# Output projection of the second block in branch halves, with a third pair of banks for the key scores

## The reference, cut to what matters

```python
mixed = jnp.concatenate([rmsnorm(o_attn, norm_attn_g[l]), rmsnorm(o_conv, norm_conv_g[l])], axis=-1)
x = x + gt1 * (mixed @ w_out[l])
h2 = rmsnorm(x, ln_ffn_g[l]) * (1 + sc2) + sh2
x = x + gt2 * peer_ffn(h2, peer_wq[l], peer_keys[l], peer_u[l], peer_v[l])

def peer_ffn(xn, w_q, sub_keys, expert_u, expert_v):
    q = (xn @ w_q).reshape(B, S, PEER_HEADS, 2, PEER_QDIM // 2)
    s = jnp.einsum('bshpd,hpkd->bshpk', q, sub_keys)
    v_half, i_half = lax.top_k(s, PEER_TOPK)
    ...
```

## Time and profile before

| | |
|---|---|
| median of 3 runs | 1239.91 us (1239.68 to 1240.51) |
| the profiled execution's own time | 1240.15 us |
| its span in the profile | 1238.4 us |
| PE busy | 1193.9 us, 96% of the span |
| DVE, ACT, POOL busy | 74%, 63%, 46% |

### The profile page before, as it was taken

How to read it: one execution, slowest core, us unless ns; L and a number is a source line. 1 busy time by engine, 2 the same in 40 slices (tenths; PEclk the granted TensorE clock), 3 DMA queues, 4 the chain that set the end, 5 groups by cost and what they waited for, 6 DMA issues and landing times.

```text
span 1238.4 us, 26652 instructions
## 1 busy us (share of the span) xinstructions
PE 1193.9 (96%) x8256; PEld 1072.4 (87%) x8256; DVE 911.3 (74%) x1885; ACT 782.6 (63%) x1784; POOL 566.6 (46%) x505
## 2 busy tenths in 40 slices
PE   8999999988897999999999999999999999999997
PEld 8888988988877999888999999998888888888886
DVE  5777768889575739997788888861676767676866
ACT  5446676465765555667887788876655555555555
POOL 3665543435464348998877777778200000000000
PEclk9999999999999999999999999999999999999999
DMA  6668656538643445565666666667676676767663
GB/s 230 228 210 298 231 196 199 170 118 302 245 126 120 134 124 173 185 187 184 195 215 209 199 201 215 201 208 270 196 243 214 193 255 194 256 193 263 188 194 109
DMA packets 85828, 249.86 MB, mean 202 GB/s; under 512 B 8019, under 2 KB 29692, under 8 KB 84988
## 3 DMA queue, kind: packets, MB, share of 16 engines
q1 hardware_dynamic: 77356, 209.62, 53.6%
q0 software_dynamic: 8400, 39.34, 8.7%
HBM read 237.38 MB, written 13.12 MB: 202 GB/s over the span
## 4 chain that ended last, share of the span: by engine, by line
PE 82%; DVE 8%; issue 4%; ACT 3%; POOL 3%; DVEq 0%; POOLq 0%; ACTq 0%
PE psum L694 81%; POOL w_lo L1644 2%; DVE w_lo L1814 1%; DVE s_sb L1828 1%; ACT w_hi L1217 1%; DVE arena L1867 1%; DVE rstd L1808 0%; ACT arena L1376 0%; ACT arena L1200 0%; PE psum L895 0%; DVE arena L2023 0%; DVE arena L1982 0%; DVE xres L1948 0%; POOL arena L1727 0%; DVE arena L1929 0%
## 5 line engine op out<-in xcount | busy, mean ns | idle before, releaser
L694 PE MATMUL psum<-h_parts,w_hi 128*128 128x256 f32 (+1 forms) x3216 | 678.0, 304 | 22.0 <-DVE w_lo L1814 8.2
L1644 POOL TENSOR_TENSOR w_lo<-ring,w_hi 128x512 fp32r<-128x512 f32 x368 | 490.8, 1346 | 275.1 <-ACT w_hi L1217 266.6
L1217 ACT ACTIVATE w_hi<-ring 128x512 fp32r<-128x512 f32 x734 | 444.9, 628 | 255.8 <-PE psum L694 244.4
L694 PEld LDWEIGHTS psum<-h_parts,w_hi 128*128 128x128 f32 x3216 | 516.6, 192 | 58.8 <-issue 24.3
L694 PE MATMUL psum<-h_parts,w_lo 128*128 128x256 f32 x1832 | 518.0, 283 | 0.0
L694 PEld LDWEIGHTS psum<-h_parts,w_lo 128*128 128x128 f32 x1832 | 350.8, 191 | 0.0
L694 PE MATMUL psum<-w_hi,h_parts 128*128 128x512 f32 (+1 forms) x1120 | 342.7, 388 | 3.8 <-DVE w_lo L1814 2.5
L694 PEld LDWEIGHTS psum<-w_hi,h_parts 128*128 128x128 f32 x1120 | 208.4, 188 | 49.5 <-issue 6.3
L1814 DVE TENSOR_TENSOR w_lo<-ring,w_hi 128x512 fp32r<-128x512 f32 x238 | 189.3, 796 | 81.6 <-ACT w_hi L1217 81.0
L694 PE MATMUL psum<-w_lo,h_parts 128*128 128x512 f32 (+1 forms) x560 | 216.3, 386 | 0.0
L2341 DVE TENSOR_TENSOR w_lo<-ring,w_hi 128x512 fp32r<-128x512 f32 x128 | 88.5, 692 | 61.6 <-ACT w_hi L1217 58.2
(11 more groups left out here) (214 smaller groups left out, 1002.3 us busy)
## 6 DMA issues: line engine op xcount, KB each, us to landing
ring<-u_t SPq DMA_DIRECT2D x128, 512.0 KB, 3.6
ring<-v_rows SPq DMA_DIRECT2D x128, 512.0 KB, 3.7
ring<-weights SPq DMA_DIRECT2D x115, 512.0 KB, 3.9
arena<-mods POOLq DMA_DIRECT2D x48, 512.0 KB, 5.3
routing_weights<-s_sb SPq DMA_DIRECT2D x32, 320.0 KB, 4.2
s_sb<-routing_weights POOLq DMA_DIRECT2D x5, 2048.0 KB, 10.3
bias_rows<-bias_row POOLq DMA_DIRECT2D x1, 1536.0 KB, 10.8
xres<-x_t SPq DMA_DIRECT2D x2, 512.0 KB, 4.6
```

The lines of the kernel that those rows point to most:

```text
L694: return nc.tensor.matmul(out, lhs, rhs, start=start, stop=stop, **kw)
L1217: nc.scalar.activation(w_hi[:, half, :], src, ACT.Copy).then_inc(hi_done, 1)
L1644: nc.gpsimd.tensor_tensor(w_lo[:, half, :], src, w_hi[:, half, :].bitcast(F32), ALU.subtract)\
```

## The change

The output projection's slots no longer hold one column block with all its rows. Each holds the convolution rows of two blocks or the attention rows of two blocks, in the order of `OUT2`. PE multiplies the convolution halves of blocks 0 to 3 first, chunk by chunk over the four blocks, then their attention halves in the same manner, and then convolution and attention halves of blocks 4 and 5 and of 6 and 7. In `mix 0` DVE now splits each convolution chunk behind the scaling of the next one, where it did all four in `mix 1`. The key scores use banks 6 and 7 for part 2.

```diff
+OUT2 = [("conv", 0), ("conv", 1), ("attn", 0), ("attn", 1), ("conv", 2), ("attn", 2), ("conv", 3), ("attn", 3)]
+OUT2_AHEAD = (3, 3, 4, 5, 6, 7, 8, 8)
...
+        def key_banks(x):
+            return psum[:, 2 + 2 * (x % 3):4 + 2 * (x % 3), :]
...
+            if s[0] == "out2":
+                branch, pair = OUT2[i]
+                for b in range(2):
+                    n_half += branch == "conv"
+                    half_free[k, b] = (half_used, n_half) if branch == "conv" else (v_done, VT[s + (2 * pair + b,)] + 1)
+                continue
...
-            pair = s[0] in ("out2", "wq") and job == 0
+            if s[0] == "out2":
+                return SPLIT[SLOT_AT[s]] + OUT2_AHEAD[job]
+            pair = s[0] == "wq" and job == 0
...
+            def out2_half(branch, blocks):
+
+                ready, first = part_ready("out2"), branch == "conv"
+                for c4 in range(4):
+                    c = c4 + (0 if first else 4)
+                    for nb in blocks:
+                        n, k = VT["out2", nb], first_wq - KC + OUT2.index((branch, nb // 2))
+                        if c4 == 0:
+                            half_ready(k, nb % 2)
+                            if first:
+                                take_v(n)
+                        ready(c)
+                        last = split_mms(vbuf(n), (2 * k + nb % 2) % 4, c4 * P, (h_hi[:, c, :], h_lo[:, c, :]),
+                                         first and c4 == 0, not first and c4 == 3)
+                        if c4 == 3:
+                            last.then_inc(half_used if first else v_done, 1)
...
-                elif kind in ("out1", "out2"):
-                    if kind == "out2":
-                        split_pair(VT["out2", 0], first_wq - KC, part_ready("out2"), take_v, v_done, (1,))
-                    for nb in range(2 if kind == "out2" else 0, KC):
...
+                elif kind == "out2":
+                    out2_half("attn", range(4))
+                    for pair in (2, 3):
+                        out2_half("conv", (2 * pair, 2 * pair + 1))
+                        out2_half("attn", (2 * pair, 2 * pair + 1))
...
-                        split_pair(VT["out2", 0], first_wq - KC, part_ready("out2"), take_v, v_done, (0,))
+                        out2_half("conv", range(4))
...
-                        if x >= 2:
-                            pe_.wait_ge(key_read, x - 1)
+                        if x == 3:
+                            pe_.wait_ge(key_read, 1)
...
                     if j:
-                        low_parts("out2", range(4))
                         dve.wait_ge(o_ready, 8)
...
-                        if c and j:
-                            low_parts("out2", (3 + c,))
+                        if c:
+                            low_parts("out2", (4 * j + c - 1,))
...
+                dve.wait_ge(key_read, 3)
                 v.tensor_copy(top_v1, top_v[:, 1, :, :]).then_inc(picked, 1)
```

More of the change, by code:

```diff
@@ L546, in block_program @@
                 half_free[k, 1] = a_done, filled(*s, i)
-            elif s[0] in ("out1", "out2"):
+            elif s[0] == "out1":
                 half_free[k, 1] = v_done, VT[s + (i,)] + 1
@@ L949, in _ @@
                             last.then_inc(v_done, 1)
-                elif kind in ("out1", "out2"):
-                    if kind == "out2":
-                        split_pair(VT["out2", 0], first_wq - KC, part_ready("out2"), take_v, v_done, (1,))
-                    for nb in range(2 if kind == "out2" else 0, KC):
+                elif kind == "out1":
+                    for nb in range(KC):
                         split_projection(VT[s + (nb,)], SPLIT[SLOT_AT[s]] + nb, part_ready(kind), take_v, v_done)
+                elif kind == "out2":
[3 more added lines that the diff above has]
+                        out2_half("attn", (2 * pair, 2 * pair + 1))
                 elif kind == "gate":
@@ L1027, in _ @@
                                 pe_.wait_ge(a_read, filled("wq", hd))
-                                last = mm(psum[:, 2 + 2 * (x % 2) + m, j * P:j * P + P],
+                                last = mm(key_banks(x)[:, m, j * P:j * P + P],
                                           blk(QP + hd)[DH * m:DH * m + DH, P * i:P * i + P],
@@ L1081, in _ @@
             for s in range(4):
-                wide_tile(s, WIDE_FROM + s, WIDE_EARLY[s], (key_read, 3) if s >= 2 else (act_read, WIDE_FROM - 1 + s))
+                wide_tile(s, WIDE_FROM + s, WIDE_EARLY[s], (key_read, 4) if s >= 2 else (act_read, WIDE_FROM - 1 + s))
             wide_tiles(WIDE_FROM + 4, SEL_TILE, WIDE_EARLY, WIDE_FROM)
@@ L1465, in _ @@
                         act.wait_ge(key_done, x + 1)
-                        banks = psum[:, 2 + 2 * (x % 2):4 + 2 * (x % 2), :]
                         nc.scalar.activation(scores_of(i)[:, :, first:first + 4, :],
-                                             banks.rearrange("p m (j k) -> p m j k", j=4), ACT.Copy)\
+                                             key_banks(x).rearrange("p m (j k) -> p m j k", j=4), ACT.Copy)\
                             .then_inc(key_read, 1)
@@ L2516, in stream @@
             out[n] = w.reshape(16, P, DH).transpose(1, 0, 2).reshape(P, D)
+        elif k == "out2":
+            branch, pair = OUT2[i]
+            rows = wo2[0:512] if branch == "conv" else wo2[512:1024]
+            out[n] = np.concatenate([cols(rows[:, P * nb:P * nb + P]) for nb in (2 * pair, 2 * pair + 1)], 1)
         else:
-            w = {"out1": x["w_out"][0], "gate": x["w_ple_gate"][0], "out2": wo2, "wq": x["peer_wq_2"][0]}[k]
+            w = {"out1": x["w_out"][0], "gate": x["w_ple_gate"][0], "wq": x["peer_wq_2"][0]}[k]
             out[n] = cols(w[:, P * i:P * i + P])
```

## The result

The changed kernel took 1244.62 us in the median of 8 runs, the kernel before 1239.80 in the median of 8. The ratio is 1.0039, with a 95% interval from 1.0029 to 1.0048: **4.8 us slower** (3.6 to 6.0). The ratios are taken over all runs of a kernel, so they can differ in the last digit from those of two medians.

A forecast was written before the change was run, and what follows sets the result against it. PE was taken to bound the kernel (82% of the span). Stage +3.73, tail +0.8, key scores -1.04 and clock +1.8 sum to +5.3 on 1239.91, so 1245.2 us; range 1241.8 to 1248.0.

The forecast's parts named there:

- Start: Ahead of the output projection: the first low split moves ahead, so PE starts at 400.34, -0.57 us.
- Attention chunks 0.6 later: In `mix 0`, alternating scalings and splits delay the attention norm's reciprocal and all that follows by 0.6 us.
- First boundary: From convolution to attention halves of blocks 0 to 3: PE waits 2.45, 0.84 and 0.98 for weights, sum 4.27 us.
- Second boundary: Ahead of the convolution halves of blocks 4 and 5: PE waits 1.45 and 0.85 for weights, sum 2.3 us.
- Tail: Behind the stage's last group: DVE's last residual starts 1.2 us behind the stage's end; +0.8, bounds 0.6 to 1.0.
- Key scores: In `route`: part 2 fills PE's 1.47 us wait for the first copy out; -1.04 us, or 0 if lost.
- The clock: In the output projection: PE's clock falls to half after the waits; +1.8 us, with 0 to 3.
- The sum for the stage: Output projection: +3.73 us from start, full-rate groups and boundary waits, plus 1.8 for slow clock.
- the first (waits and no slow clock): Output projection: the waits come but no slow clock; +3.5, 1243.4 us; chance 0.20.
- the second (the refill hidden): First boundary: weights are in place when convolution halves end, waits 0 to 1 us; 1236.8 us at zero; chance 0.06.
- the fourth (a slow clock and waits at each later boundary): Later boundaries: cover fails, 0.3 to 0.7 us each for three, slow clock at each boundary; 1248 us; chance 0.07.
- The third (taken back later): Behind the stage: a later PE wait of 3 us or more absorbs the loss; 1239.9 us; chance 0.07.

The follow-up runs named there:

- tail: The changed kernel with the last attention halves multiplied block by block (6, then 7) instead of side by side; 1244.57 us, ratio 1.0041 to the kernel before.
- after_again: The changed kernel measured once more with no edit, for a profile at the usual speed; 1246.19 us, ratio 1.0049 to the kernel before.
- late_split: The changed kernel with DVE splitting the four convolution chunks behind all four scalings again; 1244.92 us, ratio 1.0043 to the kernel before.
- key_only: The kernel before with only the third pair of banks for the key scores added; 1238.88 us, ratio 0.9996.
- pairs_ahead_tail: The changed kernel with blocks 0 to 3 in pairs, slot 2 rounded ahead of the attention chunks, last attention halves block by block; 1239.05 us, ratio 0.9993.
- early_split: The kernel before with only the moved split of the convolution chunks, each behind the next chunk's scaling; 1241.36 us, ratio 1.0010.

## Why the prediction was right

The forecast was 1245.2 us, +5.3; the two measurements are +4.8 and +6.1, with intervals that hold +5.3. Step by step, from the profile of the changed kernel:

- *Start*: forecast -0.57; PE's idle time ahead of the stage is 2.21 instead of 2.82, -0.61.
- *Attention chunks 0.6 later*: the attention norm's root is 401.17 - 396.00 = 5.17 us behind the convolution's, and before it was 400.78 - 396.46 = 4.32. That is 0.85 later where I had 1.0 for this row. ACT's last attention cast, counted in the same way, is 0.5 later, where I had 0.6.
- *First boundary*: forecast 2.45, 0.84 and 0.98; measured 2.25, 0.78 and 0.25. The last one came out small since the groups ahead of the fourth already ran at the half clock and used up most of the wait; at 0.36 per group it would have been 410.72 - 409.04 - 2 x 0.36 = 0.96. POOL's two lows took 3.01 us, as the row of before (2.99) had it. The Trainium skill ("SBUF — State Buffer", section "SBUF: two separate sides") lets either DVE or POOL hold their shared port for a whole instruction; by that the estimate for these two lows and DVE's between them is 1.29 + 0.68 + 1.29 = 3.26, and the trace is 0.25 below it.
- *Second boundary*: forecast 1.45 and 0.85; measured 1.40 and 0.80. ACT's order is part of it: the last group of block 0 starts at 416.17 and ends about 0.52 later, and the roundings start only at 417.57, behind the residual and the square of block 0. The later boundaries held: no wait behind 420.16.
- *Tail*: forecast +0.8; measured 2.95 against 428.35 - 426.22 = 2.13 before, +0.82. The size was right, and the late end of block 6 was rightly named, but the reason was incomplete: as `tail` showed, DVE's own queue stands only 0.1 behind it, so freeing the half earlier is worth 0.1 and not 0.8. The rest is block 6's residual and addition, which now stand in DVE's queue ahead of the last residual (2.88 us instead of 2.04).
- *Key scores*: forecast -1.04; 0.9 by the wait.
- *The clock*: forecast +1.8 with 0 to 3. The stage took 31.56 us, of which 23.04 are groups at full rate and 5.48 waits, so 3.04 are slow groups, against about 1.7 in the stage before. The forecast counted the waits as if all groups ran at full rate. Counted so, with 0.96 for the fourth group, they are 6.2 where it had 6.6, and what the clock adds is 31.56 - 23.04 - 6.19 = 2.3 where it had 1.8. The sum for the stage, 3.73 + 1.8 = 5.5 beside 31.56 - 25.31 - 0.61 = 5.6, is right to 0.1 since these two errors cancel, and that is luck. The place was wrong too: I had put 0.5 us of slow clock behind the first boundary and 1.3 behind the second. In `after_again` all of it came behind the first (408.8 to 415.6) and none behind the second, and `tail` and `late_split` show it at other places again.

Of the rivals, the first (waits and no slow clock) is excluded by the clock rows, the second (the refill hidden) by the waits, and the fourth (a slow clock and waits at each later boundary) by the groups behind 420.16, which follow one another without a wait at full rate. The third (taken back later) is not seen: the loss at the end of `route`, 6.45 - 0.9 = 5.6, lies within both intervals (3.6 to 6.0 and 4.3 to 7.8).

Four things stay open. The first is how much of `key_only`'s 0.9 us reaches the end. The second is how much of the loss a filler of the right length at the boundary would give back, in time and not only in one profile. The third is the price, in the tail, of DVE's addition of 1.54 us. In `tail` it starts at 428.88, beside a low of POOL that runs from 428.84 to 430.14, and ends 0.3 behind it; alone it takes 0.41. The fourth is what the second boundary would cost if ACT rounded the next halves ahead of the square of block 0. None of these was measured by itself.

## What to carry to other kernels

When a loop is widened so that more outputs share one activation chunk, count the weight buffers that it holds to its end: they come free together, and the next group wants them together, so the refill can't overlap. Take as many outputs side by side as leave one slot of buffers free for the refill, here two blocks instead of four, which took the loss from 4.8 to 1.4 us. And look at which queue does the refill: a cover for one engine's latency is worth nothing if the engine that refills stands behind the same latency in its own order. Moving the refill ahead has a price of its own, as `pairs_ahead_tail` shows: what stood there before comes later. And a difference of half a microsecond between two single profiles may be the clock's and not the edit's, so compare such profiles only beside the times of many runs.

## What the runs showed of the hardware that was not expected

The same code can meet the half clock at different places. In `after_again` it lay at 408.8 to 415.6, and in `tail`, which is the same code up to the last eight groups of the stage, at 400.7 to 404.1 and 410.9 to 414.3. The stretch differs by 0.6 us for it. In `after_again` the half clock lasted to 415.6 although PE was busy without a break from 410.7 on.

A PE that starts earlier and waits later can lose by the clock. In `early_split` the idle time was only split and moved (2.21 and 2.12 us instead of 2.82 ahead of the stage), and the slow stretch lay at 406.2 to 409.6, where PE did not wait, instead of from 402.4 on. Of the 1.65 us by which the stretch grew, 1.15 are this. It is one profile, and the time of 12 runs, +1.2 us (0.1 to 2.2), agrees with it.
